# Three post norms of a four-layer decoder run in two halves of the tokens

## The reference

```python
def rms_norm(x, w):
    xf = x.astype(jnp.float32)
    y = xf * lax.rsqrt(jnp.mean(xf * xf, axis=-1, keepdims=True) + NORM_EPS)
    return (y * w.astype(jnp.float32)).astype(x.dtype)

def sq_relu_mlp(h, w_up, w_down):
    return jnp.square(jax.nn.relu(h @ w_up)) @ w_down
...
    for i in range(DEPTH):
        j = i // N_MIXERS
        h = rms_norm(x, ln_mix_pre[i])
        if i % N_MIXERS == 0:
            m = gla_mixer(h, gla_w_in[j], gla_w_gate_up[j], gla_b_gate_up[j], gla_g_norm[j], gla_w_out[j])
        else:
            m = swa_sink_mixer(h, swa_w_in[j], swa_b_in[j], swa_sinks[j], swa_w_out[j], swa_b_out[j])
        x = x + rms_norm(m, ln_mix_post[i]).astype(x.dtype)
        h = rms_norm(x, ln_mlp_pre[i])
        f = sq_relu_mlp(h, mlp_w_up[i], mlp_w_down[i])
        x = x + rms_norm(f, ln_mlp_post[i]).astype(x.dtype)
```

## Time and profile before

| | |
|---|---|
| median of 3 runs | 2364.43 us (2364.27 to 2366.81) |
| the profiled execution | 2366.72 us, its span 2364.9 us |
| PE busy | 2339.5 us, 99% of the span |
| ACT, POOL, DVE busy | 1038.1, 978.6, 893.3 us |
| mean granted TensorE clock | 0.999 of full speed |

### The profile page before, as it was taken

How to read it: one execution, slowest core, us unless ns; L and a number is a source line. 1 busy time by engine, 2 the same in 40 slices (tenths; PEclk the granted TensorE clock), 3 DMA queues, 4 the chain that set the end, 5 groups by cost and what they waited for, 6 DMA issues and landing times.

```text
span 2364.9 us, 36347 instructions
## 1 busy us (share of the span) xinstructions
PE 2339.5 (99%) x13078; PEld 1931.7 (82%) x13078; DVE 893.3 (38%) x1802; ACT 1038.1 (44%) x1607; POOL 978.6 (41%) x497
## 2 busy tenths in 40 slices
PE   9999999999999999999999999999999999999999
PEld 6888888888878888888887978788888787888887
DVE  7975322211467743222114243311211884211212
ACT  7665444332246744434335443532332584422321
POOL 4821444444442234444443424544444414444442
PEclk9999999999999999999999999999999999999999
DMA  4311222233410012232332212222232202322221
GB/s 160 117 37 37 95 100 90 98 101 105 143 63 19 3 63 98 89 100 95 106 107 84 99 45 89 89 98 98 92 101 92 72 20 72 107 98 93 95 99 69
DMA packets 57947, 203.14 MB, mean 86 GB/s; under 512 B 7073, under 2 KB 7969, under 8 KB 57457
## 3 DMA queue, kind: packets, MB, share of 16 engines
q1 hardware_dynamic: 55440, 197.07, 25.2%
q10 hardware_dynamic: 2400, 4.63, 0.6%
HBM read 199.57 MB, written 2.10 MB: 85 GB/s over the span
## 4 chain that ended last, share of the span: by engine, by line
PE 91%; DVE 4%; POOL 2%; issue 2%; ACT 2%; DMA 0%; ACTq 0%; DVEq 0%; POOLq 0%
PE bank L807 77%; PE bank L1098 3%; PE bank L1081 2%; PE bank L1072 2%; POOL score L740 1%; DVE q_swa L2457 1%; PE bank L1204 0%; PE bank L1191 0%; PE bank L1181 0%; DVE sqacc L2373 0%; POOL w_lo L637 0%; PE bank L1064 0%; PE bank L1600 0%; DMA w_raw<-in_weights 0%; DVE tmp L2417 0%
## 5 line engine op out<-in xcount | busy, mean ns | idle before, releaser
L637 POOL TENSOR_TENSOR w_lo<-w_raw,w_hi 128x1024 fp32r<-128x1024 f32 x366 | 880.3, 2406 | 1183.6 <-ACT w_hi L1726 1171.8
L807 PE MATMUL bank<-h_hi,w_hi 128*128 128x512 f32 x1608 | 636.0, 396 | 4.5 <-POOL w_lo L637 2.6
L807 PE MATMUL bank<-h_hi,w_lo 128*128 128x512 f32 x1608 | 626.9, 390 | 0.0
L807 PE MATMUL bank<-h_lo,w_hi 128*128 128x512 f32 x1608 | 626.7, 390 | 0.0
L1726 ACT ACTIVATE w_hi<-w_raw 128x1024 fp32r<-128x1024 f32 x368 | 386.8, 1051 | 240.1 <-PE bank L807 210.3
L807 PEld LDWEIGHTS bank<-h_hi,w_hi 128*128 128x128 f32 x1608 | 302.3, 188 | 77.7 <-issue 10.2
L807 PEld LDWEIGHTS bank<-h_lo,w_hi 128*128 128x128 f32 x1608 | 302.2, 188 | 64.3 <-issue 3.1
L807 PEld LDWEIGHTS bank<-h_hi,w_lo 128*128 128x128 f32 x1608 | 302.2, 188 | 63.5
L807 PE MATMUL bank<-mact_hi,w_hi 128*128 128x512 f32 x512 | 199.4, 389 | 0.0
L807 PE MATMUL bank<-mact_hi,w_lo 128*128 128x512 f32 x512 | 199.2, 389 | 0.0
L807 PE MATMUL bank<-mact_lo,w_hi 128*128 128x512 f32 x512 | 199.2, 389 | 0.0
(11 more groups left out here) (457 smaller groups left out, 3348.7 us busy)
## 6 DMA issues: line engine op xcount, KB each, us to landing
w_raw<-in_weights SPq DMA_DIRECT2D x368, 512.0 KB, 3.3
x<-in_xT SPq DMA_DIRECT2D x4, 256.0 KB, 7.3
x<-in_xT ACTq DMA_DIRECT2D x4, 256.0 KB, 7.4
memx<-in_memT SPq DMA_DIRECT2D x1, 1024.0 KB, 10.1
cmp_w1k<-in_cmp_w ACTq DMA_DIRECT2D x1, 1024.0 KB, 5.0
cmp_w1v<-in_cmp_w ACTq DMA_DIRECT2D x1, 1024.0 KB, 6.6
out<-x SPq DMA_DIRECT2D x4, 256.0 KB, 2.1
out<-x ACTq DMA_DIRECT2D x4, 256.0 KB, 2.3
```

The source lines that it names most:

```text
L637: nc.gpsimd.tensor_tensor(w_lo[:, t % RING, :], w_raw[:, t % RAW, :], w_hi[:, t % RING, :].bitcast(F32), ALU.subtract).then_inc(lo_ready, 1)
L807: r = nc.tensor.matmul(out, a, b, start=first and n == 0, stop=last and n == 2)
```

## The change

At `mixpost0`, `mlppost0` and `mixpost1` the tokens are cut into two halves of 256 (`HALVES`). The last tile of the projection is made for the first 256 tokens, then for the last 256 (into bank 5); the sums, roots and spreads of the first half stand between the matmuls of the second. The first half of feature tiles 0 to 3 (of all 8 at `mlppost0`, `HALVED`) is scaled, added and rounded in pieces of 256 columns; the second half of these, and the other tiles whole, follow. The dummy matmuls at these three places go.

```diff
-        jobs += [(f"sum.mixpost{l}", 0)]
+        jobs += [(f"sum.mixpost{l}", 0), (f"sum.mixpost{l}.b", 0)]
...
+HALVES = [slice(0, SEQ // 2), slice(SEQ // 2, SEQ)]
+HALVED = {"mixpost0": KT // 2, "mlppost0": KT, "mixpost1": KT // 2}
+SECOND_HALF_BANK = 5
...
         @block.gpsimd
-                added(1)
+                for k in ADDED_BY_POOL:
+                    if k < HALVED[SUMMED[b]]:
+                        added(0, k)
+                added(1, 1)
                 rest_of(0)
-                added(4)
+                added(1, 4)
...
                 for name in names:
-                    end = CHUNK[FIRST[name]] + AHEAD
+                    end = CHUNK[FIRST[name]] + AHEAD - (name == "mixpre1")
                     rests(start, end)
                     start = end
                     rests_behind(name)
...
-            def two_after_post(names, norm):
-
+            def two_after_post(names, norm, between):
...
-                filler(16, tiles[0][1])
...
+                for k in range(HALVED[post]):
+                    rounded_part(0, k)
+                    if k in between:
+                        between[k]()
                 for k in range(KT):
-                    rounded_part(k)
+                    rounded_part(1, k)
...
+            def tile_in_halves(post, name, hi, lo, tiles, between):
+
+                t, b = CHUNK[name], SUMMED.index(post)
+                bank_free(JOB[name])
+                if b:
+                    pe.wait_ge(x_moved, len(STAYING) * b)
+                for h, out in enumerate((of(name), bank[SECOND_HALF_BANK])):
+                    for f in range(tiles):
+                        if h == 0 and f % KT == 0:
+                            chunk_ready(t + f // KT)
+                        if h and f in between:
+                            between[f]()
+                        r = three(out[:, HALVES[h]], slot(t + f // KT, f % KT), (hi[:, f, HALVES[h]], lo[:, f, HALVES[h]]),
+                                  f == 0, f == tiles - 1)
+                    if h == 0:
+                        r.then_inc(half_projected, 1)
+                r.then_inc(chunks_used, dict(JOBS)[name])
...
+                    tile_in_halves(apart, f"{prefix}.{KT - 1}", hi, lo, tiles,
+                                   {2: lambda: sums_of_whole_tiles(apart), 3: lambda: sums_of_half(apart, 0), 5: lambda: spread_half(apart, 0)})
...
-                    two_after_post(["sk", "sv"], "mixpre1")
+                    two_after_post(["sk", "sv"], "mixpre1", sums_then_spread("mlppost0", 3, 5))
...
-                sum_post(f"mixpost{l}")
...
+                tile_in_halves(f"mixpost{l}", f"mix{l}.{KT - 1}", *((h_hi, h_lo) if l else (gla_hi, gla_lo)), KT,
+                               {1: first_half_sums, 4: lambda post=f"mixpost{l}": spread_half(post, 0)})
...
+                loop(t0, KT // step - 1, step * per_tile, body)
+                for j in range(KT - step, KT):
+                    split_ahead(t0 + (j + 1) * per_tile - (1 if j < KT - 1 else 2))
+                    wait_evacuated(act, f"{prefix}.{j}")
...
-                round_gained(f"mlppre{l}")
+                act.wait_ge(half_projected, SUMMED.index(post) + 1)
+                square_half(0, post, of(name)[:, HALVES[0]], **biased)
+                root_half(0, post, bias=eps[:, 0:1])
...
+                round_gained(f"mlppre{l}", {0: second_square, 1: lambda: root_half(1, post, bias=eps[:, 0:1])})
...
+                    round_gained("mixpre1", {5: second_square, 6: lambda: root_half(1, "mlppost0")})
                     for k in range(KT):
                         square(k, "mixpre1", x[:, k, :])
...
-                add_normed_before(f"mixpost{l}")
+                add_normed_before(f"mixpost{l}", f"mix{l}.{KT - 1}", second_half_out, 3, 3)
...
-                    add_normed_before("mlppost0")
+                    add_normed_before("mlppost0", f"mdown01.{KT - 1}", second_half_in, 5, 7)
```

More of the change, by code:

```diff
@@ L109 @@
 OWN.update({f"sum.mlppre{l}": 3 for l in range(DEPTH)})
-OWN.update({f"inv.{name}": 2 for name in ("mixpost0", "mlppost0", "mixpost1")})
+for _name in ("mixpost0", "mlppost0", "mixpost1"):
+    OWN.update({f"sum.{_name}": 3, f"sum.{_name}.b": 3, f"inv.{_name}": 2, f"inv.{_name}.b": 3})
 OWN.update({f"got{h}.1": 5 for h in range(4)}, gatt0=5)
@@ new lines, in sums_of_whole_tiles @@
+            def sums_of_whole_tiles(post):
+                out, first = of(f"sum.{post}"), post.startswith("mlppost")
+                if first:
+                    pe.wait_ge(eps_made, int(post[-1]) + 1)
+                    for a in range(TT):
+                        nc.tensor.matmul(out[:, a:a + 1], ident[:, :], eps_out[:, a:a + 1], start=a == 0, stop=False, skip_group_check=True)
+                pe.wait_ge(sq_added, 9 * SUMS.index(post) + KT)
+                for a in range(TT):
+                    nc.tensor.matmul(out[:, a:a + 1], sqacc[:, a * P:(a + 1) * P], ones[:, 0:1], start=a == 0 and not first,
+                                     stop=False, skip_group_check=True)
@@ new lines, in sums_of_half @@
+            def sums_of_half(post, h):
+                out = of(f"sum.{post}")
+                if h:
+                    pe.wait_ge(sq_done, KT * SUMS.index(post) + KT)
+                    pe.wait_ge(post_rooted, 2 * SUMMED.index(post) + 1)
+                else:
+                    pe.wait_ge(half_squared, SUMMED.index(post) + 1)
+                for a in (2 * h, 2 * h + 1):
+                    r = nc.tensor.matmul(out[:, a:a + 1], sq[:, 1, a * P:(a + 1) * P], ones[:, 0:1], start=False, stop=True, skip_group_check=True)
+                r.then_inc(small_done, 1)
@@ L2346, in _ @@
                 else:
+                    deviation("sum.mlppost1")
                     for k in range(BY_PE):
```

225 lines of the change are left out of this document (171 added, 54 removed).

## The result

| | before | changed |
|---|---|---|
| median | 2364.42 us (2364.27 to 2366.81, 4 runs) | 2380.2 us (2378.36 to 2381.62, 4 runs) |
| ratio | 1 | 1.0061, 95% interval 1.0049 to 1.0073 |
| the profiled execution | 2366.72 us, span 2364.9 | 2379.07 us, span 2377.1 |
| mean granted clock | 0.999 | 0.996 |

The forecast was 2372.4 us (2367 to 2377). The direction was right; the loss is 12.4 us in the profiled execution and 15.8 us between the medians, where 8.0 were forecast. I walk through the trace of the changed kernel in the order of the prediction's steps.

The account below looks back on a forecast made before the run. PE was busy 99% of the span, so only waits, dummies and short operations could be won. Late sq0 weights 5.8, clock 1.7 and mix posts 0.24 each made 8.0 us slower: 2372.4 us, range 2367.0 to 2377.0.

Parts of the forecast that it names:

- Matmuls of 256 columns: At all three posts: a pair costs 0.012 us more than one of 512 columns, 1.9 us of PE time for 160.
- the other halves: At the three posts: a half operation advances ACT by about 0.40 us, DVE by 0.40, POOL by 0.70.
- the second inverse: At mixpost0: DVE can scale the second half at about 1475.3 instead of 1473.76, 1.54 us later.
- the chain behind it: At mixpost0, to tile 4's rounding: 1.30 of 6.80 us shorter, so each mix post ends 0.24 us later.
- mlppost0 to the end of its h_lo: At mlppost0: second half scaled 2.8 us later, yet h_lo ends 0.3 to 0.4 us earlier.
- The weights of sq0: Behind mlppost0: rounded only after the eight squares, so sq0 starts 6.7 us later and the copy to spare 5.8 us later.
- The clock: On sq0, after 7.4 idle us: one fall to half clock, 1.7 us lost, bounds 0 and 3.4.
- the forecast's reading of the program's end: At the program's end, where only 3 dummies follow the sums: clock mean 0.59, taken to agree that removing dummies hurts.
- Neither has room to catch up, so the 5.8 us reach the end: Behind the copy to spare: DVE busy 35.56 of 39 us, PE 37.79, so the 5.8 us delay stays.
- The posts lose their dummies and the clock falls there too: Rival, at the changed norms: two more clock falls, up to 1.7 us each, making 11.4 us, 2375.8; chance 0.14.

Follow-up runs that it names:

- e1: Changed kernel with only the two mix posts halved, mlppost0 whole with its dummies; ratio 1.0002 to the kernel before.
- e4: Changed kernel, but ACT rounds sq0's weights earlier, behind the eighth rounding of the first half, where it had been waiting; ratio 1.0019 to the kernel before.
- e6: Changed kernel with 40 dummies put in PE's wait in front of sq0; ratio 1.0047 to the kernel before.
- e3: Kernel before, whole tiles and all dummies, with only sq0's weights made late; ratio 1.0037 to the kernel before.
- e9: Kernel before, with POOL clearing 64 columns ahead of its rest of sq6's weights; ratio 1.0004 to the kernel before.
- e5: Kernel before without the 16 dummies at each of the three posts; ratio 1.0006 to the kernel before.
- e15: Changed kernel with sq0's weights in time, dummies at the halved posts, and DVE clearing 512 columns ahead of its bias of sq3; ratio 1.0018 to the kernel before.
- e16: Kernel before, with DVE clearing 512 columns ahead of its bias of sq3; ratio 1.0001 to the kernel before.

## Why the prediction was off

- *Matmuls of 256 columns, the other halves, the second inverse, the chain behind it:* right. 10.21 us for 10.2, and 0.22 and 0.24 us for 0.24 at the mix posts; e1 shows that they cost nothing to be told.
- *mlppost0 to the end of its h_lo:* right but for the clock. In e4, without a fall in it, the second half is scaled at +17.7 us as forecast, and `h_lo` ends 0.4 us earlier than before (0.3 to 0.4). Only PE did not gain by it: it is through with `sk` and `sv` at +29.93 us as before, not at the forecast +29.2 (1845.8).
- *The weights of sq0:* right in mechanism and size. e6 measures the delay of the copy at 5.81 us (5.8), e3 shows it without any half, and e4 takes it away.
- *The clock:* the step that failed most. "After 7.4 idle us I expect one such fall", 1.7 us lost. In the profiled execution there are three. Two lie before the copy and cost 4.0 us (9.81 less e6's 5.81); the third, in the attention, costs 2.0 (47.94 less e6's 45.94). The term had one fall only. The one in mlppost0's second half follows one-column passes with no wait at all; such falls stood in a rival and not in the sum, and the attention had no term. The one on sq0 was there but under-sized, 2.8 us for 1.7, since the slow stretch began during the wait and held 13 matmuls. That exactly these three came in the profiled execution is in part chance: only the one on sq0 came in every profile with the wait. And the forecast's reading of the program's end, 0.59 where only 3 dummies follow the sums, does not bear out the dummies. That fall begins in the sums ahead of them (8 passes of L1016 take 1.36 us from 2350.99 on, for 1.05 in the earlier trace rows), as e9's does, and the changed kernel has the same 3 dummies there and a clock of 1.00.
- *"Neither has room to catch up, so the 5.8 us reach the end":* true, and not enough. The stretch behind the copy grew by 2.0 us more, because the order of POOL and DVE at sq3 turned. The earlier trace rows gave busy sums; they cannot show that DVE's 35.56 us hold operations stretched by POOL, nor that 0.06 us decide which ones.
- *The rivals:* "The posts lose their dummies and the clock falls there too" (11.4 us) came nearest in number, and half by its reason: of the two falls more, one was at a halved norm amid one-column sums (`mlppost0`), the other in the attention. The mix posts kept their clock in the profiled execution; e4 shows falls there in others (25.2 us instead of 24.2). At whole tiles they made the windows 0.5 to 0.9 us longer (e5).

The sum by measured terms: 5.8 (late weights) + 6.0 (three falls) + 2.0 (the order at sq3) + 0.5 (mix posts) = 14.3 us, against 5.8 + 1.7 + 0.5. These are the ledger's own numbers, grouped by cause, so they bear on one execution and are no second proof. What stays open: what makes the clock fall in one execution and not in the next, why the weights of sq6 land some 0.1 us later behind the copy in the kernels with halves or with late weights, and how often before meets the slow order.

## What to carry to other kernels

A ring slot that is released a little later can move a rounding behind a whole block of an in-order engine: when a tile is split, look at every chunk whose slot it holds, and put the rounding into the queue where its engine waits, as e4 does. Count a clock fall for a long wait on TensorE (here some 6.4 us: a fall in six profiles of six, 1.4 to 2.9 us up to the copy in those of the halved kernels), and one with a chance for a cluster of one-column passes (3 of 13); price it only where nothing behind it waits anyway. Where GpSimd and VectorE work side by side on SBUF, look for pairs that start within 0.1 us of each other: a change elsewhere may turn them, and the two orders can differ by 2 us.

## What the runs showed that I had not expected

- Two instructions 0.06 us apart decide over 2.04 us: DVE's bias takes 2.62 us behind POOL's rest and 0.48 ahead of it, and the pair of `q_swa` 1.41 or 5.58.
- Near a tie the lock does not follow the start times of the records: in e15 POOL's rest begins 0.02 us ahead of DVE's clearing, which still takes 0.48 us, and POOL's takes 3.04 us instead of 2.39; the bias right behind it was not held up either (0.36). In e16, where POOL begins 0.14 us ahead, the clearing takes 0.48 us too, but the bias is held up (2.13) and POOL's rest is not (2.39). The clearing was held up in none of the three; what it does to the order near a tie stays open.
- Falls of the clock differ from execution to execution of one kernel: e4's profile has them at both mix posts, where the changed kernel's, with the same code there, has none.
- Dummies during a wait went with a clock of 1.00 through 6.5 us (e6), and the matmuls behind it ran at full speed, where six unfilled waits had a fall.
